# The input norm of the last layer moves from the projection stage into the end of the feed-forward stage before it

## What is computed

```python
for layer in range(2):
    h = rmsnorm(x, norm_mix[layer])
    if layer % 2 == 0:
        y = h @ ev_w_in[j]          # even: attention on y, then mix = ... @ ev_w_out
    else:
        y = h @ od_w_in[j]          # odd: sparse attention on y, then mix = ... @ od_w_out
    x = x + mix
    x = x + swiglu(rmsnorm(x, norm_ffn[layer]), w_gate, w_up, w_down)
return rmsnorm(x, norm_final)

def rmsnorm(x, g):
    return x * rsqrt(mean(x * x, axis=-1) + eps) * g
```

## Time and profile before

| | |
|---|---|
| median of three runs | 1160.29 us |
| the profiled execution | 1159.23 us, of which the span of the trace is 1157.4 us |
| PE busy | 1005.5 us, 87% of the span |
| DVE, ACT, POOL busy | 591.6, 485.2, 98.8 us |
| DMA | 228.56 MB, mean 197 GB/s |

### The profile page before, as it was taken

The page is one execution under the profiler, slowest core; times in us unless marked ns, Lnnn a source line. Parts: engine busy times, 40 slices in busy tenths (PEclk is TensorE's granted clock), DMA queues, the critical chain, the costliest instruction groups (busy, mean ns, idle before and its releaser), DMA issues. The chain is left out here.

```text
span 1157.4 us, 20084 instructions
## 1 busy us (share of the span) xinstructions
PE 1005.5 (87%) x8451; PEld 720.2 (62%) x8451; DVE 591.6 (51%) x955; ACT 485.2 (42%) x792; POOL 98.8 (9%) x111
## 2 busy tenths in 40 slices
PE   6997889978676766998888999997998888999996
PEld 5574879554333333887646777774885545777774
DVE  5574478551000001678665654546666865555443
ACT  5454354320000002554555644434545655555532
POOL 3500080000000000006000000002040000000000
PEclk9897599979778889999898999998999988999998
DMA  8822002999999996652073766633622046665530
GB/s 273 253 65 88 1 3 74 407 405 422 421 420 421 420 421 222 190 160 90 21 255 109 230 205 217 217 109 106 190 81 74 1 167 216 219 208 191 188 102 37
DMA packets 108324, 228.56 MB, mean 197 GB/s; under 512 B 7145, under 2 KB 86043, under 8 KB 93659
## 3 DMA queue, kind: packets, MB, share of 16 engines
q1 hardware_dynamic: 105275, 219.38, 52.4%
q0 software_dynamic: 2976, 8.14, 2.4%
HBM read 224.63 MB, written 1.05 MB: 195 GB/s over the span
## 5 line engine op out<-in xcount | busy, mean ns | idle before, releaser
L518 DVE SCALAR_TENSOR_TENSOR ffn_wu_lo<-ffn_w_up,ffn_wu_hi 128x2048 f16<-128x2048 f32 x44 | 99.0, 2288 | 56.0 <-ACT ffn_wu_hi L443 56.0
L1118 PE MATMUL rw_pB<-ring,kept 128*32 128x256 f32 x864 | 80.5, 479 | 42.2 <-DMA ring<-in_w_up 19.8
L656 PE MATMUL ffn_pG<-ffn_hT_hi,ffn_wu_hi 128*128 128x256 f16 x352 | 97.7, 278 | 3.4 <-DVE ffn_hT_lo L560 3.4
L656 PE MATMUL ffn_pG<-ffn_hT_lo,ffn_wu_hi 128*128 128x256 f16 x352 | 97.6, 277 | 0.0
L656 PE MATMUL ffn_pG<-ffn_hT_hi,ffn_wu_lo 128*128 128x256 f16 x352 | 97.6, 277 | 0.0
L656 PE MATMUL ffn_pU<-ffn_hT_hi,ffn_wu_hi 128*128 128x256 f16 x352 | 96.0, 273 | 0.0
L656 PE MATMUL ffn_pU<-ffn_hT_lo,ffn_wu_hi 128*128 128x256 f16 x352 | 96.0, 273 | 0.0
L656 PE MATMUL ffn_pU<-ffn_hT_hi,ffn_wu_lo 128*128 128x256 f16 x352 | 96.0, 273 | 0.0
L1118 PEld LDWEIGHTS rw_pB<-ring,kept 128*32 128x32 f32 x864 | 42.0, 137 | 76.4 <-issue 67.6
L443 ACT ACTIVATE ffn_wu_hi<-ffn_w_up 128x2048 f16<-128x2048 f32 x44 | 81.7, 1900 | 2.4 <-DMA ffn_w_up<-in_ffn_w_gate 2.3
L243 DVE SCALAR_TENSOR_TENSOR in_w_lo<-wt,in_w_hi 128x2048 f16<-128x2048 f32 (+2 forms) x22 | 52.7, 2397 | 34.9 <-ACT in_w_hi L236 34.4
(11 more groups left out here) (643 smaller groups left out, 2176.3 us busy)
## 6 DMA issues: line engine op xcount, KB each, us to landing
ring<-in_w_gate SPq DMA_DIRECT2D x27, 1024.0 KB, 26.3
ring<-in_w_up SPq DMA_DIRECT2D x27, 1024.0 KB, 26.4
ring<-in_w_down SPq DMA_DIRECT2D x26, 1024.0 KB, 26.6
ffn_w_up<-in_ffn_w_gate SPq DMA_DIRECT2D x22, 1024.0 KB, 7.6
ffn_w_up<-in_ffn_w_up SPq DMA_DIRECT2D x22, 1024.0 KB, 10.0
ffn_w_down<-in_ffn_w_down SPq DMA_DIRECT2D x22, 1024.0 KB, 5.1
wt<-in_ev_w_in SPq DMA_DIRECT2D x9, 1024.0 KB, 5.6
wt<-in_od_w_in SPq DMA_DIRECT2D x9, 1024.0 KB, 5.6
```

The source lines that it names most:

```text
L518: return nc.vector.scalar_tensor_tensor(out, whole, scale, hi, ALU.mult, ALU.subtract)
L656: ins = T.matmul(p[:, s, j * SEQ:(j + 1) * SEQ], w[:, s, m, c, j::NJ], h[:, c, :], start=(n == 0), stop=(n == 3 * KC - 1))
L1118: ins = nc.tensor.matmul(into[i * CAP:(i + 1) * CAP, 0:D_EXPERT], h[:, c, i * CAP:(i + 1) * CAP], held[:, c * D_EXPERT:(c + 1) * D_EXPERT] ...
```

## The change

`out_swiglu` gets a flag `ready`. With it, ffn2 does at its end what ffn3 does up to the roots: ACT squares each quarter when it is added, DVE makes mean and reciprocal, ACT the root. Then ACT scales token half 1 and DVE half 0 into `mix`. The projection in3 gets `mix` as its ready input, and so leaves out its own sums, roots and scaling and the load of the root table; its transposes read `mix` and wait for nothing but the barrier. The side work of in3, its DMAs and its weights are not touched, and everything before the last block of ffn2 is the same.

```diff
@@ out_swiglu, ACT @@
-                    if last:
+                    if last or ready:
                         act.wait_ge(hidden_hi, n_blocks)
                         nc.scalar.activation(end_st[:, 2, :], st[:, 2, :], ACT.Sqrt)
                         for t in range(TT):
...
                             nc.scalar.activation(end_st[:, 2, t:t + 1], end_st[:, 1, t:t + 1], ACT.Sqrt).then_inc(end_roots, 1)
+                        if ready:
+                            act.wait_ge(end_roots, TT)
+                            copy(xn[:, 1, :], x[:, 1, :], end_st[:, 2, 1:2])
@@ out_swiglu, DVE @@
                     add_final(0)
+                    if last or ready:
+                        end_recip(0)
                     if last:
-                        end_recip(0)
                         end_row_of(0)
                     add_final(1)
+                    if last or ready:
+                        end_recip(1)
                     if last:
-                        end_recip(1)
                         end_row_of(1)
+                    if ready:
+                        dve.wait_ge(end_roots, 1)
+                        nc.vector.tensor_scalar(xn[:, 0, :], x[:, 0, :], end_st[:, 2, 0:1], None, ALU.mult)
@@ odd_in @@
-        pr = Projection(nc, "in3", ctx, con, x, norm, w_in, ODD_TILES, y, first)
+        pr = Projection(nc, "in3", ctx, con, x, norm, w_in, ODD_TILES, y, first, ready=xn)
@@ hybrid_kernel @@
-            out_ffn("out2", ..., start=tile_loads("in3", w["od_w_in_2"], ODD_TILES))
+            out_ffn("out2", ..., start=tile_loads("in3", w["od_w_in_2"], ODD_TILES), ready=True)
-                odd_in(nc, con, x, a["norm_mix_2"][1], ...)
+                odd_in(nc, con, x, mix[:], a["norm_mix_2"][1], ...)
```

More of the change, by code:

```diff
@@ L355, in pair_of, with out_swiglu @@
     return wt[:, n].rearrange("p c n -> p (c n)")[:, 0:2 * D].rearrange("p (c n) -> p c n", c=2)
-def out_swiglu(nc, name, con, oT, w_out, wt, pairs_in, gain, n_blocks, w_gate, w_up, w_down, x, xn, start=(), last=None):
+def out_swiglu(nc, name, con, oT, w_out, wt, pairs_in, gain, n_blocks, w_gate, w_up, w_down, x, xn, start=(), last=None, ready=False):
     NJ = D_EXPERT // P
@@ L3195, in __init__, with odd_in @@
         self.gates = sb("gates", [P, TT, 3 * C_H])
-def odd_in(nc, con, x, norm, w_in, y, first, o, pe_emb, w1, w2):
+def odd_in(nc, con, x, xn, norm, w_in, y, first, o, pe_emb, w1, w2):
     n_tiles = len(ODD_TILES)
@@ L3697, in hybrid_kernel, with out_ffn @@
                               scratch, keep, start=tile_loads("in2", w["ev_w_in_2"], EVEN_TILES))
-        def out_ffn(out_name, w_out, name, layer, oT, start=(), last=None):
+        def out_ffn(out_name, w_out, name, layer, oT, start=(), last=None, ready=False):
             up = lambda m: (lambda e: m[layer].rearrange("(p c) n -> p c n", p=P)[:, :, bass.ds(e * D_EXPERT, D_EXPERT)])
@@ L3703, in out_ffn @@
             out_swiglu(nc, name, con, oT, w_out, wt, arrived_of[out_name], a["norm_ffn_2"][layer], D_FF // D_EXPERT,
-                       up(a["ffn_w_gate_2"]), up(a["ffn_w_up_2"]), down(a["ffn_w_down_2"]), x, mix, start=start, last=last)
+                       up(a["ffn_w_gate_2"]), up(a["ffn_w_up_2"]), down(a["ffn_w_down_2"]), x, mix, start=start, last=last, ready=ready)
         with ExitStack() as even:
@@ L3713, in hybrid_kernel @@
                 even_attention(nc, con, y, e, low, evenT, start=pair_loads("out2", w["ev_w_out_2"]))
-            out_ffn("out2", w["ev_w_out_2"], "ffn2", 0, evenT, start=tile_loads("in3", w["od_w_in_2"], ODD_TILES))
+            out_ffn("out2", w["ev_w_out_2"], "ffn2", 0, evenT, start=tile_loads("in3", w["od_w_in_2"], ODD_TILES), ready=True)
         with ExitStack() as odd:
@@ L3721, in hybrid_kernel @@
                 o = OddTiles(inner, nc)
-                odd_in(nc, con, x, a["norm_mix_2"][1], w["od_w_in_2"], y, first["in3"], o, w["od_cmp_pe_2"], w["od_cmp_w1_2"],
+                odd_in(nc, con, x, mix[:], a["norm_mix_2"][1], w["od_w_in_2"], y, first["in3"], o, w["od_cmp_pe_2"], w["od_cmp_w1_2"],
                        w["od_cmp_w2_2"])
```

## The result

The changed kernel is slower. Over 20 runs each its median is 1165.94 us, that of the kernel before 1160.58 us; the ratio is 1.0049, with a 95% interval of 1.0029 to 1.0069, which is 3.4 to 8.0 us. I had forecast 1161.8, with a range up to 1163.4, and gave "slower by over 0.2%" one chance in four. The profiled execution took 1164.96 us (span 1163.2), against 1159.23 (span 1157.4).

What follows compares the result with a forecast made beforehand. PE was busy 87%, but in3's chain from tile 2's arrival was taken to decide: arrival +1.5 us, PE's 2.1 us sooner start spent waiting, so 1160.29 + 1.5 = 1161.8 us; range 1159.0 to 1163.4.

Steps and rivals of the forecast that it cites:

- The new end, the border and the moved starts: ffn2 to in3: last work +2.78 us, border 1.02, in3 2.78 later, transposes 2.1 sooner, SP's tile 2 request unchanged.
- The waits that I named: In in3, PE's 2.1 us gained at the start are spent waiting, at `rows_in` or for tile 2.
- How the two queues share: In in3, about 45 packets of tile 2 per engine enter before `oi_w1s`'s second half, so tile 2 arrives at 813.6.
- my own 1.8 us: Forecast's delay from POOL issuing a load of `oi_w1s`'s size to its first bytes (797.69 to 799.5).
- L2: Arrival of tile 2 in in3, forecast to move from 812.12 to 813.6, by +1.5 us.
- tile 2 last of all: Rival in in3: engines take both `oi_w1s` halves before serving q1 again; arrival 814.9, +2.8 us, 1163.1 us; chance 0.25.
- Nothing gives it back: In in3, the wait before `oi_xp` follows tile 2's arrival by +1.5 us, and later work does not recover it.
- Behind it PE runs without a gap in the trace up to the next border, so nothing gives it back: After the wait before `oi_xp`: PE has no gap up to the next border, so the +1.5 us stays in the total.
- my cases: Whole forecast: +0.5 to +2.2 us (0.42), tile 2 last (0.25), first or nearly (0.24), gain kept (0.09).

Runs made afterwards that it cites:

- e1: Changed kernel with POOL's five side loads of in3 issued ahead of its four memsets; median 1157.45 us, ratio to the kernel before 0.9987.
- f1: Changed kernel with seven extra matmuls into an unread buffer at the very end of in3; median 1163.83 us, ratio to the kernel before 1.0043.
- e4: Kernel before with an extra 2.74 us POOL memset ahead of its side loads in in3; median 1172.82 us, ratio to the kernel before 1.0104.
- e7: Changed kernel with `oi_w1s` loaded by SP at the end of ffn2 into a used-up weight's room; median 1157.24 us, ratio to the kernel before 0.9996.
- e8: Kernel before with `oi_w1s` loaded by SP at the end of ffn2 into a used-up weight's room; median 1161.27 us, ratio 1.0022.
- f3: Changed kernel with `oi_w1s` loaded by SP at ffn2's end and seven extra matmuls at in3's end; median 1156.44 us, ratio to the kernel before 0.9972.
- e2: Changed kernel with both halves of `oi_w1s` issued only when tile 2 has landed; median 1169.64 us, ratio to the kernel before 1.0098.
- e3: Kernel before with both halves of `oi_w1s` issued only when tile 2 has landed; median 1169.49 us, ratio to the kernel before 1.0104.
- r4: Kernel before run again unchanged, for a third trace; profiled execution 1158.45 us.

## Why the prediction was wrong

**The new end, the border and the moved starts: right.** ACT's scaling ended 6.03 behind the second addition (6.05 forecast), the border took 0.98 (1.02), in3 started 2.70 later (2.78), the transposes 2.12 sooner (2.1), SP asked for tile 2 11.27 behind the second addition (11.28), POOL issued its first half 3.08 behind the stage's start (3.08). The waits that I named are there: `rows_in` with 0.54, tile 2 with 3.02.

**How the two queues share: wrong in size.** I read from the earlier trace rows that some 58 packets per engine stand in what a queue has put in hand (counted from 7.6 on, though by my own 1.8 us the small load stood ready only at 8.0), and so placed the first 45 of tile 2 ahead of the second half of `oi_w1s`. There were 11 ahead of the equal sharing, and L2 moved by +2.66 instead of +1.5. What the earlier trace rows show is how long a small load waits behind a queue that is already at work; it does not say that a tile asked for in the middle of another load gets that far ahead. The right anchor was in the same paragraph: both queues served packet for packet, as the earlier trace rows have it, from the moment on when both have work. With it the whole second half moves along with tile 2, and since its packets are few and large it is done first; tile 2 ends last, as in the rival "tile 2 last of all", whose price (+2.8) is the one measured, though its mechanism (q0 alone until it is done) is not. The Trainium skill, "DMA: Bandwidth & Descriptors", section "Queues, rings and completion order", has an engine take a whole packet of 9 to 17 descriptors from one queue before it turns. By that rule L2 would have come to +2.2, nearer than my +1.5. The counts of 229 against 311 in 4 us, 14 and 19 per engine, don't tell how long a turn is.

**"Nothing gives it back": right in in3.** From `w_hi` of tile 2 to the matmuls on `oi_xp` passed 16.49 us (16.67 before), and from there to the attention 45.55 both times. e1 and f1 show the same: tile 2 moves by 0.75 and 2.57, the attention's start by 0.63 and 2.51. In e4 the matmuls on `oi_xp` start 2.82 later, and the low clock from there on adds the rest of its 9.23; in e7, e8 and f3, where nobody waits for tile 2, the attention moves by 1 us less than its split.

**"Behind it PE runs without a gap in the trace up to the next border, so nothing gives it back": the step that failed.** True up to the border, it was taken for the whole rest: I let the shift of in3 pass through the attention unchanged, and so put the clock's part at nothing without a reason. The attention itself took 4.2 us longer, as PE had half its clock for a long stretch. None of my cases had this. The page's own row of granted clocks lay before me, with PEclk under 9 in 15 of 40 slices, and the trace of before has a low stretch at 881.3, just behind the same border: I should have asked what becomes of that stretch when the stage moves, and given it a chance and a price of some 4 us.

How much of the measured 5.4 us between the medians is this? The traces say 2.5 for in3 and 4.2 for the clock, three executions against three. The timed runs say the same by another way. The mean granted clock was 0.9207 over the changed kernel's runs and 0.9255 over 73 runs of the kernel before (those taken beside the experiments), and among the runs of one kernel 0.01 of clock goes with 6.8 us. So, as an estimate, 0.0048 of clock are 3.3 of the 5.9 us between the two means; at equal clock the changed kernel stays 2.6 us slower, give or take 1.1, near in3's share. How far to trust this count the others show: it gives -2.7 for e7, -3.0 for f3 and -0.8 for e8, whose attention starts 2.9, 2.9 and 1.1 us sooner by the traces, but -1.5 for e1, where it starts 0.6 later. For f1 it leaves 2.4 us, as the trace has it, but f1's clock of 0.9211 is no better than the changed kernel's: it is there that the trace and the timed runs disagree. That the low clock costs the time is shown; that PE's pause at the border sets it off rests on f1's trace, and is not shown. The Trainium skill, "TensorE: Matmul & The Clock Gate", section "Part 1: The HAM clock gate (the "warmup" mystery)", says that a gate sets the clock by how busy TensorE has been lately, to one level or the other. The rows of the windows agree with two levels, 1.00 and 0.50. Low clock followed PE's pauses of 3.02 us at tile 2 and of 5.29 in e2, as such a gate would have it. But behind the same pause it can come or not: 3.74 us ahead of ffn3's first matmuls before and in e7, and 1.79 ahead of the attention, behind which the long stretch stood in three executions of the changed kernel and in none of before. What decides between them, the runs leave open.

## What to carry to other kernels

When a stage starts later on one engine and its transfers are asked for by two, list both queues' loads with their new times. Where they overlapped here, the one with many small packets ended last, and moving a load behind a tile only handed the wait to the next tile (e2, e3). Side loads go ahead of memsets in the order of the engine that issues them, which was worth 1.9 us of in3 in e1. And before a stage is moved by a few microseconds, look at the granted clock at the next place where TensorE pauses or works thinly: a low stretch there can grow by more than the move was meant to bring. And one trace of each kernel is too few to tell such a stretch from a loss that the change makes each time.

## What the runs showed of the hardware

- Two kernels that differ by 2.5 us in when a stage starts differ by 4.2 us in how long it takes, at the same instructions and the same pause of 1.79 us ahead of it; e8, 1.11 sooner than before, pays it too in its one trace.
- What a stretch of low clock costs depends on where it falls. With the one at 881.3 to 884.5 and without it (r4) the attention took 80.5 us to ffn3's first addition; without the one at 932.4 it took 79.0 (e1), and without that at 942.6 too 77.9 (e7). The long ones cost 4.2 (attention) and 4.7 to 5.0 us (the matmuls on `oi_xp` alone, 12.21 and 12.42 instead of 7.47).
- PE was at half its clock although the profile has it busy 13.30 of 13.30 us in that stretch: being busy by the profile did not bring the clock back at once.
- A VectorE operation on two columns that began beside a GpSimd memset of 2.74 us ended only with it, after 2.56 us instead of 0.17 (e4, one trace).
- The 73 runs of the kernel before lay between 1147.3 and 1168.7 us and their mean granted clock between 0.914 and 0.941; the time follows the clock with a correlation of -0.91, so most of the spread goes with it. Twenty runs of each kernel left an interval of 4.6 us for this change.
